# Sums over the v rows of the first tile moved into the u stage, and 96 dot products with u rows moved into the last stage

## The reference, cut to what matters

```python
def peer_ffn(xn, w_q, keys1, keys2, u, v):
    ...
    def blk(xb):
        q = (xb @ w_q).reshape(TOK_BLOCK, PEER_HEADS, PEER_KEY_DIM)
        s1 = jnp.einsum('thd,hnd->thn', q[..., :half], keys1).astype(jnp.float32)
        s2 = jnp.einsum('thd,hnd->thn', q[..., half:], keys2).astype(jnp.float32)
        v1, i1 = lax.top_k(s1, PEER_TOPK)
        v2, i2 = lax.top_k(s2, PEER_TOPK)
        ...
        g = jax.nn.softmax(sv, axis=-1)
        h = jax.nn.gelu(jnp.einsum('td,thkd->thk', xb, u[eidx]).astype(jnp.float32), approximate=False)
        return jnp.einsum('thk,thkd->td', (g * h).astype(v.dtype), v[eidx])
```

## Time and profile before

| what | value |
|---|---|
| three runs | 3956.85, 3968.24 and 3971.69 us; median 3968.24 |
| the profiled execution | 3969.84 us, of it 3968.0 us span |
| mean granted TensorE clock | 0.95 |
| busy share of the span | PE 88%, DVE 62%, POOL 49%, ACT 29% |

### The profile page before, as it was taken

How to read it: one execution, slowest core, us unless ns; L and a number is a source line. 1 busy time by engine, 2 the same in 40 slices (tenths; PEclk the granted TensorE clock), 3 DMA queues, 4 the chain that set the end, 5 groups by cost and what they waited for, 6 DMA issues and landing times. The chain is left out here.

```text
span 3968.0 us, 49765 instructions
## 1 busy us (share of the span) xinstructions
PE 3478.3 (88%) x17237; PEld 2501.8 (63%) x17237; DVE 2448.6 (62%) x5652; ACT 1158.6 (29%) x2264; POOL 1944.2 (49%) x1478
## 2 busy tenths in 40 slices
PE   7889887998989898887877878898689999999998
PEld 4445555788978676765666666665455556656655
DVE  3764423655857677779879697897633444434344
ACT  1213323121156523222222222266622212222222
POOL 0000001224400144778888888854267777877773
PEclk9888987998999999999999999999899999999999
DMA  2002103312431235799999999979998998989995
GB/s 117 10 33 61 55 27 123 101 54 87 140 96 33 85 121 191 278 348 377 399 396 401 400 396 401 374 253 400 329 366 324 363 360 336 392 339 351 358 374 217
DMA packets 335403, 978.48 MB, mean 247 GB/s; under 512 B 34400, under 2 KB 84456, under 8 KB 333648
## 3 DMA queue, kind: packets, MB, share of 16 engines
q0 software_dynamic: 156672, 570.49, 36.7%
q1 hardware_dynamic: 173584, 389.78, 27.9%
q10 hardware_dynamic: 4928, 15.34, 1.1%
HBM read 873.61 MB, written 101.89 MB: 246 GB/s over the span
## 5 line engine op out<-in xcount | busy, mean ns | idle before, releaser
L1606 PE MATMUL n_ps<-n_xh_flat,n_wh 128*128 128x512 f32 x3072 | 748.3, 401 | 162.8 <-POOL n_wh L1596 160.9
L2884 PE MATMUL e_y_ps<-e_wh,e_vh 128*128 128x512 f32 x3072 | 751.3, 401 | 45.4 <-DVE e_wh L3008 34.7
L1606 PEld LDWEIGHTS n_ps<-n_xh_flat,n_wh 128*128 128x128 f32 x3072 | 581.3, 192 | 325.2 <-POOL n_wh L1596 202.9
L2884 PEld LDWEIGHTS e_y_ps<-e_wh,e_vh 128*128 128x128 f32 x3072 | 572.1, 189 | 266.6 <-issue 130.4
L1025 POOL CAST m_wh<-raw 128x1024 fp32r<-128x1024 f32 x40 | 42.2, 1054 | 911.4 <-issue 659.0
L2968 POOL TENSOR_TENSOR e_vh<-raw,e_vh 128x1024 fp32r<-128x1024 f32 x128 | 309.2, 2418 | 225.9 <-ACT e_vh L2910 223.0
L3047 DVE TENSOR_TENSOR oT<-e_y_ps,oT 128x512 f32<-128x512 f32 x256 | 175.8, 691 | 376.0 <-PE e_y_ps L2884 303.6
L2543 POOL DMA_INDIRECT e_rows<-in_v,eid x346 | 349.1, 1009 | 99.0 <-issue 86.9
L1596 POOL TENSOR_TENSOR n_wh<-raw,n_wh 128x1024 fp32r<-128x1024 f32 x128 | 307.4, 2402 | 39.6 <-ACT n_wh L1591 37.3
L1943 DVE CUSTOM_DVE_ANT_0 oT<-oT,n_row_ps 128x1024 f32<-128x1024 f32 x227 | 270.9, 1217 | 67.9 <-DMA oT<-in_u,eid 64.4
L1062 PE MATMUL m_ps<-m_xh_flat,m_wh 128*128 128x272 f32 x1920 | 261.8, 298 | 40.7 <-DVE oT L1095 12.3
(11 more groups left out here) (390 smaller groups left out, 5698.1 us busy)
## 6 DMA issues: line engine op xcount, KB each, us to landing
raw<-in_ut SPq DMA_DIRECT2D x128, 512.0 KB
raw<-in_v SPq DMA_DIRECT2D x126, 512.0 KB
s_hid<-flat SPq DMA_DIRECT2D x128, 256.0 KB
xrow<-s_hid SPq DMA_DIRECT2D x126, 256.0 KB
s_gate<-g_stage SPq DMA_DIRECT2D x3, 8192.0 KB, 53.1
raw<-in_w_pq SPq DMA_DIRECT2D x32, 512.0 KB
m_ring<-s_gate SPq DMA_DIRECT2D x32, 512.0 KB
gh<-s_gate SPq DMA_DIRECT2D x32, 512.0 KB
```

Source lines behind the costliest of these rows:

```text
L1606: mm = pe.matmul(self.ps[:, n % 2, 0:ND], self.uh[:, at % 2, a, k * P:(k + 1) * P], self.xd[:, b, k, :], start=(k == 0 and o == 0), stop=( ...
L2884: mm = pe.matmul(y_ps[:, o, 0:TD], vh[:, n % SLOT, a, m * P:(m + 1) * P], wh[n % SLOT][:, b, g * TD:(g + 1) * TD], start=(c == 0 and e == ...
```

## The change

Four things are done together.

1. The 32 batches of the first tile (128 gathers of v rows and 32 sums) run in the u stage, one for each 3.2 blocks from block 22 on. Their weights need the dots of tile 0 complete, so all 128 of these dots are made in the dense mixer. The sum is kept in DRAM and read back in the last stage.
2. The last 96 dots (64 of tile 3 and the 32 of the sample) are made in the last stage, with their own gathers and three row buffers, and their weights are placed when they are done.
3. The two PSUM banks that held x now hold the sum of the first tile. The dots read x from SBUF: from `xrow` and from a second tile `r_x_row`, which SyncE loads in turn. `show_rows` is gone.
4. One routing slot more stands in the u stage (slots 4 to 8, before 5 to 8), and the chunk sizes are new. The ring of u rows has 10 buffers, before 14; the v rows have 8 in the last stage, before 13.

```diff
-CHUNKS_AT = (0, 0, 0, 0, 0, 18, 32, 32, 30, 12, 4)
+FIRST_IN_U = 4
+CHUNKS_AT = (0, 0, 0, 0, 28, 22, 22, 22, 21, 9, 4)
-DOTS_AT = (0, 0, 0, 64, 64, 128, 128, 128, 32, 0)
+DOTS_AT = (0, 0, 128, 64, 64, 64, 64, 64, 0, 0)
-N_DOT = NSP
+N_LAST = 96
+N_DOT = NSP - N_LAST
+WEIGH_AT, GELU_BLOCK, TURN_BLOCK, SUM_FROM, SUM_TO = (3, 8), 12, 18, 22, 122
+SUM_BLOCKS = tuple(SUM_FROM + b * (SUM_TO - SUM_FROM) // 31 for b in range(32))
...
         def dot(d):
 
-            dve.wait_ge(row_shown, d // P + 1)
+            i = d // P
+            if i > 0:
+                dve.wait_ge(x_loaded[i % 2], 16 * ((i + 1) // 2))
             b = ring.take(now[0])
             dve.wait_ge(row_ready[b], 16 * ring.uses(d))
-            dve.tensor_tensor_reduce(out=rows[b], in0=rows[b], in1=row_flat,
+            dve.tensor_tensor_reduce(out=rows[b], in0=rows[b], in1=x_rows[i % 2],
...
+        x_rows = [xrow[:, :], sb("x_row", [P, D])[:, :]]
...
                 for n in chunks(j):
                     hidden.product(pe, n)
+                    if n == TURN_BLOCK:
+                        pe.wait_ge(weighed, 1)
+                        pe.matmul(w_ps, hn[:, 0:P], ident, start=True, stop=True).then_inc(weights_turned, 1)
+                    for b in range(32):
+                        if SUM_BLOCKS[b] == n:
+                            at = [(4 * b + g) % N_ROW for g in range(4)]
+                            sums.sum(pe, b, [v_rows[i] for i in at], [v_row_ready[i] for i in at],
+                                     [16 * ((4 * b + g) // N_ROW + 1) for g in range(4)])
...
-            def show_rows(i):
-
-                if i > 0:
-                    act.wait_ge(x_loaded, 16 * i)
-                    act.wait_ge(dotted, i * P)
-                act.activation(row_flat, xrow[:, :], ACT.Copy).then_inc(row_shown, 1)
...
-            for j in range(5, QT + 2):
+            for j in range(FIRST_IN_U, QT + 2):
                 first = done[0]
                 for i, n in enumerate(chunks(j)):
                     if n + 2 < NKEY:
                         hidden.split(pool, n + 2)
-                    last = min(DOTS_TO[j] + 10, N_DOT)
+                    last = max(first, min(DOTS_TO[j] + 7, N_DOT))
                     gathers(first + -(-(last - first) * (i + 1) // CHUNKS_AT[j]))
+                    while batch < 32 and GELU_BLOCK < n and SUM_BLOCKS[batch] <= n + 6:
+                        for g in range(4):
+                            i_row = 4 * batch + g
+                            if i_row >= N_ROW:
+                                pool.wait_ge(sums.summed, (i_row - N_ROW) // 4 + 1)
+                            sums.gather(pool, batch, g, v_rows[i_row % N_ROW], v_row_ready[i_row % N_ROW])
+                        batch += 1
...
 def slot_of(s):
 
-    return C_FIRST + (s - B_STEPS) * (C_LAST - C_FIRST) // (LAST_IN - B_STEPS) if s <= LAST_IN else N_SLOT
+    if s > LAST_IN:
+        return N_SLOT
+    if s > BEFORE_LAST:
+        return LAST_SUMS + (s - BEFORE_LAST - 1) * (C_LAST - LAST_SUMS) // (LAST_IN - BEFORE_LAST - 1)
+    return C_FIRST + (s - B_STEPS) * (LAST_GELU - C_FIRST) // (BEFORE_LAST - B_STEPS + 1)
+
+
+def dot_slot(d):
+
+    return 4 + (d - N_DOT) * 50 // (C0 - N_DOT) if d < C0 else 58 + (d - C0) * 24 // T_S
...
+            def gather_last(d):
+
+                i = d - N_DOT
+                if i >= N_LAST_ROW:
+                    pool.wait_ge(last_dotted, i - N_LAST_ROW + 1)
+                pool.indirect_dma_start(out=last_rows[i % N_LAST_ROW], out_offset=None, in_=dram["u"],
+                                        in_offset=bass.IndirectOffsetOnAxis(ap=eid[:, d:d + 1], axis=0)
+                                        ).then_inc(last_ready[i % N_LAST_ROW], 16)
...
+            def dot_last(d):
+
+                i = d - N_DOT
+                row = last_rows[i % N_LAST_ROW]
+                dve.wait_ge(x_loaded, 16 if d < C0 else 32)
+                dve.wait_ge(last_ready[i % N_LAST_ROW], 16 * (i // N_LAST_ROW + 1))
+                dve.tensor_tensor_reduce(out=row, in0=row, in1=x_row, scale=1.0, scalar=0.0, op0=ALU.mult, op1=ALU.add,
+                                         accum_out=hn[:, d:d + 1]).then_inc(last_dotted, 1)
```

More of the change, by code:

```diff
@@ L1987, in keep_ids, with weigh_first @@
             n_eid[0] += 1
+        def weigh_first():
+            dve.wait_ge(kept, 1)
+            dve.scalar_tensor_tensor(out=idt0[:, :], in0=routes[:, 0, 0:P], scalar=float(NKEY), in1=routes[:, 1, 0:P],
+                                     op0=ALU.mult, op1=ALU.add).then_inc(idt_ready, 1)
+            dve.memset(sums.zero[:, :, :], 0.0).then_inc(sums.cleared, 1)
+            dve.wait_ge(gelued, 1)
+            dve.wait_ge(gn_ready, 1)
+            dve.tensor_tensor(hn[:, 0:P], hn[:, 0:P], gn[:, 0:P], ALU.mult).then_inc(weighed, 1)
         def slot(j):
@@ L2204, in route @@
         rows = [keep[part][:, a + i * D:a + (i + 1) * D]
-                for part, a, n in (("ring", 0, RING), ("oS_flat", 2 * D, 2), ("oD_flat", 0, 4), ("q_flat", 0, 4))
+                for part, a, n in (("ring", 0, RING), ("oS_flat", 2 * D, 2), ("oD_flat", 0, 4))
                 for i in range(n)]
+        sums.wz = keep["q_flat"][:, 0:2 * 544].rearrange("p (a n) -> p a n", a=2)
+        mk, mv = (keep[n][:, :, :].rearrange("p a n -> p (a n)") for n in ("mk_p", "mv_p"))
+        v_rows = [part[:, a + i * D:a + (i + 1) * D] for part, a, n in ((keep["q_flat"], 2 * 544, 4), (mk, 0, 2), (mv, 0, 2))
+                  for i in range(n)]
         hidden = DenseHidden(mx, keep, dram, mx.xh)
@@ L2451, in _ @@
         def _(pool):
+            for past in late_sems:
+                pool.sem_clear(past)
             done = [0]
@@ L2492, in _ @@
                 hidden.split(pool, n)
-            for j in range(5, QT + 2):
+            batch = 0
+            for j in range(FIRST_IN_U, QT + 2):
                 first = done[0]
@@ L2658, in _ @@
                         at = [(4 * b + g) % N_ROW for g in range(4)]
-                        sums.sum(pe, b, [rows[:, i, :] for i in at], [row_ready[i] for i in at],
-                                 [16 * ((4 * b + g) // N_ROW + 1) for g in range(4)])
+                        sums.sum(pe, B_FIRST + b, [rows[:, i, :] for i in at], [row_ready[i] for i in at],
+                                 [16 * (rows_before + (4 * b + g) // N_ROW + 1) for g in range(4)])
         @block.gpsimd
@@ L2740 @@
 SLOT = 2 * CG
-NBUF = 13
+N_LAST_ROW = 3
 NY = KD * NGD
@@ L2866, in turn_sum, with turn_last @@
                 mm.then_inc(sum_turned, 1)
+            def turn_last():
+                pe.wait_ge(last_weighed, 1)
+                pe.wait_ge(sum_added, 4)
+                pe.matmul(sums.ps[:, 1, 0, C0 - P:C0], hn[:, C0 - P:C0], ident, start=True, stop=True)
+                for q in range(4):
+                    part = slice(q * 32, (q + 1) * 32)
+                    mm = pe.matmul(sums.ps[part, 1, 1, 0:T_S], hn[:, C0:NSP], ident[:, part], start=True, stop=True)
+                mm.then_inc(last_turned, 1)
             for p in range(NPH):
@@ L2991, in _ @@
                     done = max(done, goal)
+                    while next_dot < NSP and dot_slot(next_dot) <= 4 * p + i + 2:
+                        gather_last(next_dot)
+                        next_dot += 1
             for b in range(done, N_BATCH):
```

275 lines of the change are left out of this document (165 added, 110 removed).

## The result

The changed kernel takes **4162.0 us** (median of 4 runs, 4154.6 to 4174.7) against 3968.1 of before. The ratio is 1.050, 95% interval 1.046 to 1.053. The forecast was 3997, with a range up to 4060: the sign held, the size did not. The profiled execution has a span of 4172.9 us (it is the slowest of the four runs, 13 us over the median), before 3968.0.

A forecast was written before the change was run, and what follows sets the result against it. It took POOL's queue to bound the u stage and PE the last stage. Terms -68 (last stage), -28 (POOL), +99 (port), +30 (dense mixer), -4 (between stages) sum to +29: 3997 us from the median, range 3862 to 4060.

The forecast's parts named there:

- the -23 for `show_rows`: U stage: with `show_rows` gone, POOL's waits for ACT ahead of the tail go, -23 us.
- the last stage's -68: Last stage: 32 batches leave, -83 us, less +15 for transfers and fewer row buffers; together -68, bounds -83 and -41.
- the hand layout of dots and gathers: One u-stage period laid out: first gather behind the split +0.95 us, next two +0.05 each, 1.05 us in a period.
- +99 in the u stage: U stage: two-SBUF-input dots and POOL shut each other out, 0.85 us over 116 blocks, +99 us, bounds 0 and +162.
- 2 x 14 in the dense mixer: Dense mixer: contention of dots with POOL, 0.85 us a block over two groups of 16 blocks, 14 us each.
- -28 in the u stage: U stage, POOL without contention: fewer gathers -30, `show_rows` -23, tail +24, weight memsets +1; together -28 us.
- The term for the tail: U stage, last 11 splits: no gathers behind them, so PE's 5.47 us a block decides instead of POOL, +24 us.
- the 1.75 us between 5.47 and 7.22: U stage: room between PE's block time and POOL's period, claimed to hide PE's sums of 1.85 us each.
- the +15: Last stage: part of the 83 us not kept, for heavier transfers and row buffers going from 13 to 8, +15 us.
- B: Rival: the dots, a custom DVE operation, don't take the shared port; -98 us, 3870 us; chance .20.
- C: Rival: dots take the port cheaply, some 0.35 us a block, 52 us in place of 127, 3922 us; chance .15.
- D: Rival: DVE becomes the bound, 1.4 us a block, 207 us in place of 127, 4077 us; chance .15.

The follow-up runs named there:

- the one-input run: The changed kernel with each of its 544 dots replaced by a reduction that reads the gathered row alone, without the product with x: 3972.4 us, 1.0016.
- the spread run: The changed kernel with one-input reductions for dots and the 128 u-stage gathers of v rows spread, one or two behind each split: 3961.2 us, 0.9988.
- the first experiment: The kernel before with one edit, x copied into an SBUF tile instead of the two PSUM banks: 4182.1 us, 1.055.

## Why the prediction was wrong

The two halves of the forecast can be checked apart, since the one-input run is nearly the change without the port: the forecast for that was -98 us and then +127 of contention, sum +29. By the spans the runs gave +6 and +199. So the larger miss, 104 us, lies in what the change was to earn, and 72 lie in the port. Three steps failed: the -23 for `show_rows`, the last stage's -68, in which DVE's time and the port have no term, and the hand layout of dots and gathers.

**The port, right in kind, too small.** The mechanism that the forecast named makes the difference between the changed kernel and the one-input run (but for the reads of the accumulator), and in the kernel before it alone makes 1.055. By the step "+99 in the u stage" it was 120 us (1061.9 against 941.9). By the step "2 x 14 in the dense mixer" it was 49: the 128 gathers there have a mean of 1.43 us, in the one-input run 0.99. And the last stage had no such term, where it was 29: there the forecast let the dots run beside POOL as if they had one input. The step that failed in the first two is "The next two gathers meet dots that begin in their gaps: +0.05 each". The timeline above shows the opposite: while dots run back to back, a gather that starts with or in one waits for its end, and the next, 0.3 us later, meets another one. Of the signs, the gathers' mean over 1.1 us and the dots' long maximum came true (4.4 us even, instead of 3.6); splits of over 2.6 did not (2.53).

The Trainium skill's rule ("SBUF — State Buffer", "Who interferes with whom") that a DVE instruction with two SBUF inputs blocks a GpSimd one that reads SBUF, and one with a single input does not, agrees with the traces here: splits and dots wait for each other in the changed kernel, and the one-input reductions stay within 1.23 us. Its inference that descriptor generation would be spared by a `tensor_tensor` does not hold: beside a plain two-input operation one gather took 2.02 us, and beside these dots gathers went from 0.95 to 1.38 us, 201 us in all, while splits went up by 0.05. The measurement decides, as the forecast let it.

**-28 in the u stage without the port: it was +19.** POOL's 448 gathers in the stage took 555 us with their gaps in the one-input run, against 577 for 473 before: -22, where -30 was forecast. The term for the tail was right: POOL waited 33 us for ACT there, before 12, so +21 where +24 was forecast. What failed is "`show_rows` is gone": with it the 23 us of waits ahead of the tail were to go. `show_rows` went, and they rose to 38, so the term is 38 us off. 12 us of the wait come from the bursts of seven gathers (the spread run). The forecast let the 1.75 us between 5.47 and 7.22 hide the sums of v rows; that holds for the mean of blocks, and by this run not for each of them. The stores behind the routing load are worth some 7 us in the kernel before. The rest of the 38, some 20 us, I can't assign.

One reading of the forecast was wrong without harm: the profile does count the 0.3 us between two gathers as idle. the groups of gathers in POOL's u stage have 126 us of idle time in front of them, beside the 37.7 in front of the splits. The period of 7.22 us has these gaps in it, so the 1.21 us for a gather stand.

**-68 in the last stage: it was -31 without the port, -2 with it.** The removal of the batches was sized about right: with hardly any work in the dots it was -56. The forecast counted the dots for transfers and gave DVE's time no price, without a reason; DVE was busy for 465 of 1093 us before. But DVE runs in order, and the output adds that PE waits for stand behind the dots. That cost 25 us, and the second input 29. The forecast's own sign for this, a last stage that keeps less than 40 us, came true, but its cause for it, transfers, is not what the runs show: with all transfers in place and hardly any work in the dots the stage keeps 56. The change of the ring from 13 to 8, for which I had left something in the +15, costs nothing in the kernel before.

**+2 in the dense mixer and -4 between the stages** were +11 and +1 in the one-input run, and 5 us came behind the last product, for which there was no term.

**The rivals.** B was refused by the first experiment: the custom operation takes the port. C's price of a block, 0.35 us, is too low: in the kernel before it is 1.5 us, in the changed one 120 / 128 = 0.9 in the u stage. D's 207 us of contention are near the 199 of the runs, but by luck: DVE is busy for 751 of the u stage's 1065 us, less than the 785 of 923 before, and POOL waits there for dots to free a buffer for less than 1 us. The range ended at 4060 because every case took the -98 as sure and varied only the port. A case in which nothing was earned, with the port at its upper bound, would have reached 3968 + 207 = 4175.

## What to carry to other kernels

An operand's memory is a cost: before a tensor moves from PSUM to SBUF to make room, look at what the engine that shares the port does meanwhile, and price it for every one of its instructions that can meet the moved one. Sum the parts of a change that earn time with the same doubt as those that cost it; here the gain of each freed queue went to the next wait (POOL's for ACT, PE's behind DVE's order). And try the parts alone: the one that only moved dots to where POOL stood idle gains 1%, the four together lose 5%.

## What the runs showed of the hardware

- A dot of 128x1024 with one operand in PSUM stayed within 1243 ns and let gathers take 0.95 us; the same operation with both operands in SBUF had a maximum of 3.7 to 4.5 us, with gathers of 1.38 us in the mean in the kernel before with x in SBUF and 1.25 in the changed one. A reduction of the same size with one SBUF input is like the first.
- A gather held up this way ended 0.81 to 0.82 us after the DVE operation that held it (three gathers: 1825.52 before, 2204.81 and 2207.16 after).
- The issue of the store behind a load of 1 MB in SP's queue (r_pqt) took 3.47 us where its neighbours took 0.32 to 0.43, and ACT waited 8.8 us for a store to land; with the load issued by ACT these waits of ACT, 28.7 us, were gone.
- Over 600 us of the last stage in one run the DMA share was 0.98 to 0.99 at 367 to 378 GB/s, with PE busy for 93 to 96%; in the u stage of before it was 1.00 at 384.
